# A hybrid layer with a mixture of experts on one core: shorter start, fewer small matrix products, zero rows sent in two parts, and another order of the last layer norm

## The chip, the core and the metric

The kernel runs on one core of one Trainium2 chip. The time is the device time of one execution in microseconds (us). The engines are named as the profile does: PE is TensorE, DVE is VectorE, ACT is ScalarE, POOL is GpSimd, SP is SyncE, which here only issues transfers. A transfer is issued on the queue of an engine and carried by the core's 16 DMA engines.

## The reference

One layer over T = 384 token rows of D = 1024, held as three tiles of 128: one tile is the context pass (stream 0), two are the sample (stream 1), to which a position embedding is added first. In short:

```python
sh1, sc1, g1, sh2, sc2, g2 = split(silu(c) @ w_ada + b_ada, 6)      # per stream
xs = x_sample + pos
z = (x * (1 + sc1) + sh1) @ w_in + b_in      # 11 groups of 512, and 16 gate columns
y_r = gelu(r_g) * (rglru forward + backward over conv(r_x))
y_h = head_rms(hgrn2 forward + backward(g_q, g_ff, g_fb, g_i)) * silu(g_o)
y_m = sigmoid(m_o) * head_ln(mlstm forward + backward(m_q, m_k, m_v, m_g))
x = layer_norm(ALPHA * x + g1 * (concat(y_r, y_h, y_m) @ w_out), ln1_g, ln1_b)
h = x * (1 + sc2) + sh2
f = sum over the 2 chosen of 16 experts: w * (silu(h @ w_gate) * (h @ w_up)) @ w_down
out = layer_norm(ALPHA * x + g2 * f, ln2_g, ln2_b)
```

The mLSTM needs, for each of 4 heads and 2 directions, the row of running maxima m_t over time, spread over all partitions. The expert stage takes each token row to two slots of a table `slot_rows` of 16 x 384 rows in DRAM; slots that no token takes must hold zeros. The final states of the three mixers are outputs too.

## The kernel before

**Large products.** All are made in three fp32r products: a weight piece of 512 columns, 2 MiB in DRAM, is split into w_hi (ACT, line 803 in the mixer, 1027 in the experts) and w_lo = w - w_hi (DVE, lines 1676 and 2130), 128x1024 at a time, and PE adds h_hi w_lo, h_lo w_hi and h_hi w_hi through the helper `mm` (line 1128). In the mixer the 24 pieces of `PIECES` pass through a ring of three slots, `ring`; SP sends a piece as soon as its slot is free (line 510). Pieces 0 and 1 are the ada groups 0 and 2 of w_ada (shift and scale of the first modulation), 2 is rx, 3 gq, 4 gff, and so on; 20 is mo, 21 to 23 are w_out.

**The order.** `schedule()` writes out a list of jobs; every engine walks through it and does its part of each job. So a job's place in the list sets what stands ahead of it on all of PE, ACT and DVE. The jobs that matter here:
- `ada_row g`: silu(c) times ada group g, 8 matmuls of 32x512 on PE (four column groups side by side, each over two of eight k), and one ACT copy to `ada_rows`; its four partial rows lie on different partitions.
- `ada_col g`: turns the row into columns and adds the partials: 4 matmuls of 128x2 with `stream_sel` (line 1128, out ps, in small,extra). There are 12 of these pairs.
- `xT i half`: PE transposes x (line 1244) for tile i; for the sample it waits for the position embedding, which DVE adds (line 1638, 128x2048).
- `h`, `tile k`, `first k`: DVE's columns of the modulation, ACT's modulated k-th eighth of hT (line 849), and the first part of rx.
- `gates`: the 16 gate columns, for y (i or f) and direction d 4 columns each: 32 matmuls of 4x384 at depth 128.
- `rows1`, `rows2`: DVE's work on the gate rows (36x384), with scans; it ends in the row of maxima, MR.
- `ml_rows n`: one matmul that spreads head h, direction d of MR over 128 partitions, plain fp32 with a depth of 4, eight of them.

**Zero rows.** SP sends 12 slices of 2 MiB from `zero_tile` to `slot_rows` (line 543) between pieces, as `ZERO_AFTER` says. ACT's job `take 6` overwrites the unit in which `zero_tile` lies, and waits for all twelve. POOL waits for all twelve before it scatters the token rows (six indirect DMAs, line 729).

**Small loads.** At the start POOL's queue carries x, pos and the gate weights ahead of the small weights of the RG-LRU. After the mixer POOL sends in one burst x again, pos, the rows of the second modulation, ln_g, ln_b, constants (`iota` last), and then, when the state C is out, the two g2 rows (512 KB each, line 705).

**The experts.** 16 experts run in pairs, 6 MiB of weights each; at the last one PE, ACT and DVE read `over` (how many rows the fullest expert has) and jump over two more passes that are not needed here.

**The tail.** ACT scales the rows that POOL has picked from the first of the two experts (line 1119); DVE adds the second and g2 (lines 2205 to 2207); for each tile PE mixes the last expert's rows with the picked ones into PSUM (from 740.60 us); DVE multiplies by g2 (line 2211), adds to x (2212), takes the statistics (1953, 1954), ACT takes a root (1122), DVE applies it (1956 to 1958), and SP sends the tile out.

## Time and profile before

| | us |
|---|---|
| median of 3 runs | 777.58 (777.57 to 777.61) |
| the profiled execution | 776.95 |
| its span, first to last instruction | 775.2 |
| PE busy | 703.2 (91%), mean granted clock 0.962 |
| DVE busy | 577.0 (74%) |
| ACT busy | 432.2 (56%) |
| POOL busy | 58.5 (8%) |
| moved by DMA | 220.06 MB, 284 GB/s |

The stages by time: start to 33, mixer to 345, out projection, first norm and routing to 441, experts to 736, tail to 775.2. Busy shares are averages over stages with different limits; the clock is given in parts of full speed.

### The profile page before, as it was taken

Reading aid. Unit: us, or ns where it says so; the run is one execution under the profiler, and the core shown is the slowest. Engines: PE = TensorE matmul, PEld = TensorE weight load, DVE = VectorE, ACT = ScalarE, POOL = GpSimd, SP = SyncE. Lnnn points to the kernel's source line nnn. Section 1 sums busy time; section 2 is a strip of 40 time slices with the busy share of each in tenths; the row PEclk is TensorE's granted clock in tenths of the full one; section 3 lists DMA queues with packets and bytes.
Section 4 is the critical chain, followed back from the end, with each engine's and each line's share of the span. In section 5 each row is a group of like instructions: output and inputs, shape, how many; then the busy total and the mean of one; then the engine's idle time right before and its main releaser. Section 6 shows DMA issues by size and latency. Waiting matters only on the chain.

```text
span 775.2 us, 12312 instructions
## 1 busy us (share of the span) xinstructions
PE 703.2 (91%) x4722; PEld 553.5 (71%) x4722; DVE 577.0 (74%) x834; ACT 432.2 (56%) x597; POOL 58.5 (8%) x90
## 2 busy tenths in 40 slices
PE   3699999799999989999996999999999999999870
PEld 1477998698778969884453877888888888788630
DVE  2549697667995344573596988998999998999675
ACT  1546867245124344761122368888888888888510
POOL 4050000000010000024000300000000000000400
PEclk9799999899999989999998899999999999999986
DMA  9995599989665650319704999999999999999521
GB/s 331 359 299 199 210 333 384 374 321 401 256 231 177 229 218 5 109 30 163 305 1 148 404 402 394 398 398 399 400 400 400 399 399 399 399 399 381 168 80 54
DMA packets 91507, 220.06 MB, mean 284 GB/s; under 512 B 3335, under 2 KB 3631, under 8 KB 91455
## 3 DMA queue, kind: packets, MB, share of 16 engines
q1 hardware_dynamic: 84512, 197.66, 68.2%
q0 software_dynamic: 6528, 21.56, 9.1%
q8 instruction: 33, 0.54, 0.3%
q10 hardware_dynamic: 415, 0.14, 0.1%
q14 instruction: 19, 0.16, 0.1%
HBM read 179.99 MB, written 39.36 MB: 283 GB/s over the span
## 4 chain that ended last, share of the span: by engine, by line
PE 68%; DVE 11%; DMA 9%; ACT 4%; issue 4%; POOL 2%; SPq 0%; DVEq 0%; ACTq 0%; POOLq 0%
PE ps L1128 65%; DMA ring<-in_w_ada 3%; DMA iota<-in_consts 3%; DMA arena<-in_w_up 2%; PE ps L1515 1%; DMA slot_rows<-arena,small 1%; PE ps L1534 1%; POOL slot_rows L729 1%; DMA ring<-in_w_gate 1%; ACT w_hi L1027 1%; DVE w_lo L1676 1%; ACT w_hi L803 1%; DVE small L1953 1%; DVE picked_rows L2211 1%; DVE arena L1957 1%
## 5 line engine op out<-in xcount | busy, mean ns | idle before, releaser
L2130 DVE TENSOR_TENSOR w_lo<-arena,w_hi 128x1024 fp32r<-128x1024 f32 x96 | 114.7, 1221 | 12.3 <-ACT w_hi L1027 11.5
L2130 DVE TENSOR_TENSOR w_lo<-ring,w_hi 128x1024 fp32r<-128x1024 f32 x96 | 114.8, 1221 | 9.3 <-ACT w_hi L1027 8.4
L1027 ACT ACTIVATE w_hi<-ring 128x1024 fp32r<-128x1024 f32 x96 | 100.5, 1063 | 21.7 <-PE ps L1128 18.9
L1027 ACT ACTIVATE w_hi<-arena 128x1024 fp32r<-128x1024 f32 x96 | 100.8, 1065 | 17.9 <-PE ps L1128 13.7
L1128 PE MATMUL ps<-h_hi,w_lo 128*128 128x384 f32 x288 | 103.6, 360 | 6.2 <-DVE w_lo L1676 4.7
L1128 PE MATMUL ps<-w_hi,slot_tokens_lo 128*128 128x512 f32 x256 | 102.6, 401 | 0.8 <-DVE w_lo L2130 0.8
L1128 PE MATMUL ps<-w_hi,slot_tokens_hi 128*128 128x512 f32 x256 | 100.2, 391 | 0.0
L1128 PE MATMUL ps<-w_lo,slot_tokens_hi 128*128 128x512 f32 x256 | 99.8, 390 | 0.0
L1128 PE MATMUL ps<-h_lo,w_hi 128*128 128x384 f32 x288 | 98.8, 343 | 0.0
L1128 PE MATMUL ps<-h_hi,w_hi 128*128 128x384 f32 x288 | 98.6, 342 | 0.0
L1676 DVE TENSOR_TENSOR w_lo<-ring,w_hi 128x1024 fp32r<-128x1024 f32 x44 | 53.7, 1225 | 30.1 <-ACT w_hi L803 29.0
L1128 PE MATMUL ps<-arena 128*32 128x32 f32 (+5 forms) x1576 | 61.7, 229 | 8.4 <-issue 7.4
L1128 PEld LDWEIGHTS ps<-h_hi,w_lo 128*128 128x128 f32 x288 | 55.9, 194 | 12.6 <-issue 9.3
L1128 PE MATMUL ps<-ring,arena 128*128 128x512 f32 x144 | 64.5, 607 | 0.0
L803 ACT ACTIVATE w_hi<-ring 128x1024 fp32r<-128x1024 f32 x44 | 46.1, 1051 | 33.0 <-PE ps L1128 32.1
L1128 PEld LDWEIGHTS ps<-arena 128*32 128x32 f32 (+3 forms) x1576 | 46.6, 123 | 22.5 <-issue 16.6
L875 ACT ACTIVATE arena<-ps,small 128x384 f32<-128x384 f32 x32 | 18.5, 579 | 71.9 <-PE ps L1128 71.8
L1128 PEld LDWEIGHTS ps<-h_lo,w_hi 128*128 128x128 f32 x288 | 56.2, 195 | 0.6
L1128 PEld LDWEIGHTS ps<-h_hi,w_hi 128*128 128x128 f32 x288 | 55.8, 194 | 0.0
L1128 PEld LDWEIGHTS ps<-w_hi,slot_tokens_lo 128*128 128x128 f32 x256 | 48.1, 188 | 10.8 <-issue 1.5
L1128 PEld LDWEIGHTS ps<-w_hi,slot_tokens_hi 128*128 128x128 f32 x256 | 48.0, 188 | 10.3
L1128 PEld LDWEIGHTS ps<-w_lo,slot_tokens_hi 128*128 128x128 f32 x256 | 48.2, 188 | 9.0
(352 smaller groups left out, 1115.9 us busy)
## 6 DMA issues: line engine op xcount, KB each, us to landing
slot_rows<-arena SPq DMA_DIRECT2D x12, 2048.0 KB, 17.0
ring<-in_w_in SPq DMA_DIRECT2D x11, 2048.0 KB, 11.5
ring<-in_w_ada SPq DMA_DIRECT2D x10, 2048.0 KB, 10.1
ring<-in_w_gate SPq DMA_DIRECT2D x8, 2048.0 KB, 18.3
ring<-in_w_up SPq DMA_DIRECT2D x8, 2048.0 KB, 19.2
ring<-in_w_down SPq DMA_DIRECT2D x8, 2048.0 KB
arena<-in_w_gate SPq DMA_DIRECT2D x8, 2048.0 KB, 18.4
arena<-in_w_down SPq DMA_DIRECT2D x8, 2048.0 KB, 15.1
```

The costliest lines, as they stand in the source:

```text
L729: pool.indirect_dma_start(slot_rows, bass.IndirectOffsetOnAxis(row_i[:, NT * c + i:NT * c + i + 1], 0), H2[:, i, :], None).then_inc(S["dis ...
L803: act.activation(part_unit(w_hi, u % 4, col), raw_unit(p % NSLOT, u % 4, col), ACT.Copy).then_inc(S["hi_ready"], 1)
L875: act.activation(chunk(dst_of[g], c), bank[:, 0:T], ACT.Gelu_apprx_tanh if g == "rg" else ACT.Identity, bias=bias).then_inc(S["z_taken"], 1)
L1027: act.activation(w_hi[:, at_ % 4, :], raw[:, q * QUARTER:(q + 1) * QUARTER], ACT.Copy).then_inc(S["hi_ready"], 1)
L1128: return pe.matmul(out, lhsT, rhs, start=start, stop=stop, skip_group_check=open_)
L1515: last = pe.transpose(ps[:, half, k * P:(k + 1) * P], XG[b][:, (4 * half + k) * P:(4 * half + k + 1) * P], ident)
L1534: last = pe.transpose(ps[:, 2, k * P:(k + 1) * P], AC[:, k * P:(k + 1) * P], ident)
L1676: tt(lo, raw, hi.bitcast(F32), ALU.subtract).then_inc(S["lo_dve"], 1)
L1953: step(dve.bn_stats(mv_stats[:, 6 * half:6 * half + 6], x[:, half * 512:(half + 1) * 512]))
L1957: step(stt(x, x, mv_stats[:, 12:13], ln_b[:, v, :], ALU.subtract, ALU.mult))
L2130: tt(w_lo[:, at_ % 4, :], raw[:, q * QUARTER:(q + 1) * QUARTER], w_hi[:, at_ % 4, :].bitcast(F32), ALU.subtract).then_inc(S["lo_dve"], 1)
L2211: step(tt(y[:, cols], ps[:, bank, :], g2_b[:, s, cols], ALU.mult))
```

## The change

1. **Start.** x, pos go on SP's queue behind piece 1; the gate weights go behind the small RG-LRU weights on POOL's. In `schedule()`, `ada_row 2`, both `ada_col` and `h 0` come ahead of the transposes; DVE adds pos in two halves behind `h 0`.
2. **Small products.** `ada_row` is 16 matmuls of 32x256, so that its partials lie on two column groups and two row groups; `ada_col` is 2 matmuls of 128x4. `gates 0` is 8 matmuls of 16x384 into four column groups, copied by ACT to `gate_sums`; `gates 1`, behind gq[0], adds and places them with 4 matmuls of 4x384. `ml_rows` is one fp32r matmul over `max_parts` (the maxima as a high and a low part, made by DVE at the end of rows2).
3. **Zero rows.** Five slices stay early and have a semaphore of their own, for which `take 6` waits; seven go out late, from `zero_late`, which POOL clears when the HGRN2 final state is done: one behind piece 20, two behind each w_out piece.
4. **g2.** The two g2 loads and the wait for C stand behind the six scatters.
5. **Tail.** `over` is read before the last down product; where no further pass is needed, ACT scales the picked rows ahead of the last expert's two output copies; the statistics are a sum that comes with the addition (DVE) and a square with a sum (ACT); the three tiles are interleaved. The job itself, mixing on PE, is as before.

The diff, cut:

```diff
-ZERO_AFTER = {4: 1, 6: 1, 8: 1, 9: 1, 10: 1, 11: 1, 12: 2, 13: 2, 14: 1, 15: 1}
+ZERO_AFTER = {4: 1, 6: 1, 8: 1, 15: 2}
+ZERO_LATE = {20: 1, 21: 2, 22: 2, 23: 2}
...
-    steps = [("cond",), ("ada_row", 0), ("rows",)] + [("xT", 0, half) for half in range(2)] + [("ada_row", 2)]
-    steps += [("xT", i, 0) for i in range(1, NT)] + [("ada_col", 0), ("ada_col", 2), ("h", 0)]
+    steps = [("cond",), ("ada_row", 0), ("rows",), ("ada_row", 2), ("ada_col", 0), ("ada_col", 2), ("h", 0)]
+    steps += [("xT", 0, half) for half in range(2)] + [("xT", i, 0) for i in range(1, NT)]
...
-    steps += [rx[0], rx[1], ("conv", 0), rx[2], rx[3], ("conv", 1), ("gates",), ("conv", 2)]
-    steps += [gq[0], ("lru_mm", 0), ("conv", 3), gq[1], ("lru_mm", 1), ("rows1",), gq[2], ("lru_act", 0), ("lru_den", 0)]
+    steps += [rx[0], rx[1], ("conv", 0), rx[2], rx[3], ("conv", 1), ("gates", 0), ("conv", 2)]
+    steps += [gq[0], ("gates", 1), ("lru_mm", 0), ("conv", 3), gq[1], ("lru_mm", 1), ("rows1",), gq[2], ("lru_act", 0), ("lru_den", 0)]
...
                     piece(n, ada_v[:, :, name * G:(name + 1) * G], KD)
+                    if n == 1:
+                        sp.dma_start(x_in[:, 0, :], a["x_prompt"][0]).then_inc(S["x_in"], 16)
+                        sp.dma_start(x_in[:, 1:3, :], a["x_sample"][0].rearrange("(i p) d -> p i d", p=P)).then_inc(S["x_in"], 16)
+                        sp.dma_start(pos_in, a["pos"].rearrange("(i p) d -> p i d", p=P)).then_inc(S["pos_in"], 16)
...
+            sp.wait_ge(S["zero_tile"], 2)
+            for _ in range(ZERO_LATE[20]):
+                zero_rows(zero_late, "in_zeroed")
             for n in range(3):
                 slot_free(WOUT[n])
                 piece(WOUT[n], a["w_out"][0, n * G:(n + 1) * G, :].rearrange("(k p) n -> p k n", p=P), C)
+                for _ in range(ZERO_LATE[WOUT[n]]):
+                    zero_rows(zero_late, "in_zeroed")
...
             pool.wait_ge(S["hg_final"], 1)
+            pool.memset(zero_late, 0.0).then_inc(S["zero_tile"], 1)
...
-            pool.wait_ge(S["out_C"], 16)
-            modulation([g2_b[:, s, :] for s in range(2)], 3, "g2_in")
-
-            pool.wait_ge(S["in_zeroed"], 16 * 12)
+            pool.wait_ge(S["zeroed_first"], 16 * ZERO_FIRST)
+            pool.wait_ge(S["in_zeroed"], 16 * (12 - ZERO_FIRST))
             pool.wait_ge(S["route_ready"], 1)
             for i in range(NT):
                 for c in range(2):
                     pool.indirect_dma_start(slot_rows, bass.IndirectOffsetOnAxis(row_i[:, NT * c + i:NT * c + i + 1], 0),
                                             H2[:, i, :], None).then_inc(S["dispatched"], 16)
+
+            pool.wait_ge(S["out_C"], 16)
+            modulation([g2_b[:, s, :] for s in range(2)], 3, "g2_in")
...
-                    for r in range(2):
+                    for kk in range(4):
                         for j in range(4):
-                            k = 4 * r + j
-                            last = mm(bank[32 * j:32 * j + 32, :], silu_w[:, 2 * k:2 * k + 32], w[k], r == 0, r == 1)
+                            k, cols = 4 * (j % 2) + kk, slice(256 * (j // 2), 256 * (j // 2) + 256)
+                            last = mm(bank[32 * j:32 * j + 32, 0:256], silu_w[:, 2 * k:2 * k + 32], w[k][:, cols], kk == 0, kk == 3)
...
-                    for c in range(4):
-                        last = mm(bank[:, 2 * c:2 * c + 2], ada_rows[:, b, c * P:(c + 1) * P], stream_sel)
+                    for x in range(2):
+                        last = mm(bank[:, 4 * x:4 * x + 4], ada_rows[:, b, x * P:(x + 1) * P], group_sel)
...
+                    if job[1] == 0:
+                        pe.wait_ge(S["gate_w_in"], 16)
+                        for r in range(2):
+                            for j in range(4):
+                                k = 4 * r + j
+                                last = mm(bank[32 * j:32 * j + 16, 0:T], gate_w[:, k, :], hT[:, k, :], r == 0, r == 1)
+                    else:
...
-                                last = mm(bank[at_:at_ + H, 0:T], gate_w[:, k, c0:c0 + H], hT[:, k, :], k == 0, k == KD - 1)
+                                last = mm(bank[at_:at_ + H, 0:T], ident_blocks[:, c0:c0 + H], gate_sums)
...
-                    r = slice(32 * d, 32 * d + H)
-                    mm(ps[:, 3, 0:T], ident[r, 32 * d + h:32 * d + h + 1].broadcast_to([H, P]), MR[r, :]).then_inc(S["bc_ready"], 1)
+                    mm(ps[:, 3, 0:T], row_sel[0:64 + HR, 4 * d + h:4 * d + h + 1].broadcast_to([64 + HR, P]),
+                       max_parts[0:64 + HR, :]).then_inc(S["bc_ready"], 1)
...
+                    step(dve.tensor_copy(max_hi, MR))
+                    step(tt(max_parts[64:64 + HR, :], MR, max_hi.bitcast(F32), ALU.subtract))
+                    step(dve.tensor_copy(max_parts[0:HR, :], max_hi.bitcast(F32)), "m_rows")
...
+            with act.Else():
+                first_picked()
+                out_rows_sb(NE - 1, NPAIR - 1, 1, True)
+            act.activation(rstd, eps, ACT.Sqrt)
             for i in range(NT):
                 act.wait_ge(S["ln_var"], NT + i + 1)
-                act.activation(rstd, mv_stats[:, 13:14], ACT.Sqrt, bias=eps).then_inc(S["ln_std"], 1)
+                act.activation(PICK[:, 1, i, :], X1[:, i, :], ACT.Square, bias=row_mean[:, i:i + 1], accum_out=row_sq[:, i:i + 1]).then_inc(S["ln_std"], 1)
+                act.wait_ge(S["ln_std"], NT + 2 * i + 1)
+                act.activation(row_rstd[:, i:i + 1], row_sq[:, i:i + 1], ACT.Sqrt, bias=eps, scale=1.0 / D).then_inc(S["ln_std"], 1)
...
+                step(stt(X1[:, i, :], X1[:, i, :], 1.0, y, ALU.mult, ALU.add, accum_out=row_mean[:, i:i + 1]))
+                step(ts(row_mean[:, i:i + 1], row_mean[:, i:i + 1], -1.0 / D, None, ALU.mult), "ln_var")
...
+                step(stt(x, x, row_mean[:, i:i + 1], ln_b[:, 2, :], ALU.add, ALU.mult))
+                step(dve.reciprocal(row_rstd[:, i:i + 1], row_rstd[:, i:i + 1]))
+                step(stt(x, x, row_rstd[:, i:i + 1], ln_b[:, 3, :], ALU.mult, ALU.add), "out_tile")
...
+            mixed_rows(0)
+            mixed_rows(1)
+            result(0)
+            mixed_rows(2)
+            result(1)
+            result(2)
```

How it moves instructions, at three places.

PE at the start of the program, before. `ring,silu_w` is an ada_row, `small,extra` are ada_col, line 1244 are transposes of x, `h_hi,w_lo` begins the large products:

```order
L1128 MATMUL ps<-ring,silu_w 32x512 x8
L1235 MATMUL ps<-small,arena 128x128
L1236 MATMUL ps<-small,arena 128x56
L1244 MATMUL ps<-small,arena 128x128 x8
L1128 MATMUL ps<-ring,silu_w 32x512 x8
L1244 MATMUL ps<-small,arena 128x128 x8
L1128 MATMUL ps<-small,extra 128x2 x8
L1128 MATMUL ps<-h_hi,w_lo 128x384
```

The same place now (line 1169 is `mm`, 1287 the transposes):

```order
L1169 MATMUL ps<-ring,silu_w 32x256 x16
L1276 MATMUL ps<-small,arena 128x128
L1277 MATMUL ps<-small,arena 128x56
L1169 MATMUL ps<-ring,silu_w 32x256 x16
L1169 MATMUL ps<-small,extra 128x4 x4
L1287 MATMUL ps<-small,arena 128x128 x16
L1169 MATMUL ps<-h_hi,w_lo 128x384
```

Both ada_row and ada_col now stand ahead of all transposes, which stand directly before the first large product.

SP late in the mixer, before. `slot_rows<-arena` is a slice of zero rows, the others are weight pieces:

```order
L510 DMA ring<-in_w_in 128x8x512
L543 DMA slot_rows<-arena 1024x1x512
L510 DMA ring<-in_w_ada 128x8x512 x3
L510 DMA ring<-in_w_in 128x8x512 x2
L510 DMA ring<-in_w_out 128x4x1024 x3
L554 DMA ring<-in_w_gate 128x8x512
```

And now:

```order
L521 DMA ring<-in_w_ada 128x8x512 x3
L521 DMA ring<-in_w_in 128x8x512 x2
L542 DMA slot_rows<-arena 1024x1x512
L521 DMA ring<-in_w_out 128x4x1024
L542 DMA slot_rows<-arena 1024x1x512 x2
L521 DMA ring<-in_w_out 128x4x1024
L542 DMA slot_rows<-arena 1024x1x512 x2
L521 DMA ring<-in_w_out 128x4x1024
L542 DMA slot_rows<-arena 1024x1x512 x2
L578 DMA ring<-in_w_gate 128x8x512
```

Seven slices now stand between and behind the three w_out pieces, the last two ahead of the first expert's weights.

POOL before the experts, before. `mod_rows` are the g2 rows, `slot_rows` the six scatters:

```order
L718 DMA b_router<-in_b_router 128x16
L719 DMA tri<-in_consts 128x128
L720 DMA desc_95<-in_consts 128x16
L721 DMA iota<-in_consts 128x128
L705 DMA arena<-mod_rows 128x1024 x2
L729 DMA slot_rows<-arena,small 6144x1024 x6
```

And now:

```order
L740 DMA b_router<-in_b_router 128x16
L741 DMA tri<-in_consts 128x128
L742 DMA desc_98<-in_consts 128x16
L743 DMA iota<-in_consts 128x128
L749 DMA slot_rows<-arena,small 6144x1024 x6
L727 DMA arena<-mod_rows 128x1024 x2
```

The two g2 loads have changed places with the six scatters.

## Rows read from the trace of the kernel before

**Rows 1.** Windows: us, busy (instructions) of each engine, PE clock, DMA share, GB/s

```profile
0.00:35.00 35.00, 14.87 (x73) 8.42 (x73) 11.30 (x23) 11.44 (x22) 7.83 (x16) 0.88 0.98 356
50.00:112.00 62.00, 60.73 (x378) 52.26 (x377) 51.72 (x109) 44.88 (x67) 0.56 (x1) 1.00 0.71 248
112.00:206.00 94.00, 86.50 (x1456) 75.40 (x1456) 70.80 (x100) 41.01 (x59) 0.00 (x0) 0.96 1.01 374
...
281.00:345.00 64.00, 61.39 (x366) 55.49 (x365) 38.97 (x94) 36.21 (x79) 5.86 (x17) 0.95 0.23 83
...
417.00:465.00 48.00, 38.76 (x221) 33.54 (x221) 41.51 (x84) 24.85 (x29) 7.54 (x6) 0.89 1.01 384
```

**Rows 2.** Chain that ended last, its start: start, us, what

```profile
1.33 20.70 DMA ring<-in_w_ada
...
31.48 1.24 DVE w_lo L1676
32.81 1.30 PE ps L1128 x3
```

**Rows 3.** Timeline, the start, DVE and PE: start, us, engine line, form

```profile
18.08 2.29 DVE L1638 TENSOR_TENSOR arena<-arena 128x2048 f32<-128x2048 f32 x1 [10.45 <-DMA arena<-in_pos]
...
24.85 1.90 PE L1244 MATMUL ps<-small,arena 128*128 128x128 f32 x8
```

**Rows 4.** PE: timeline (gates), groups (busy, mean ns), chain (111.83)

```profile
59.80 5.34 PE L1128 MATMUL ps<-arena 128*4 128x384 f32 x64
...
L1128 PE MATMUL ps<-small,extra 128*128 128x2 f32 x96 | 11.5, 243 | 0.8 <-issue 0.8
...
L1128 PE MATMUL ps<-arena,small 4*128 4x384 f32 x16 | 7.3, 532 | 1.7 <-ACT arena L977 1.7
...
111.83 8.22 PE ps L1128 x50
```

**Rows 5.** Stretch 60 to 112, DVE's timeline, and ACT's w_hi from the chain

```profile
61.24 1.23 DVE L1676 TENSOR_TENSOR w_lo<-ring,w_hi 128x1024 fp32r<-128x1024 f32 x1
...
89.36 0.56 DVE L1755 TENSOR_SCALAR arena<-arena 128x768 f32<-128x768 f32 x1 [5.38 <-ACT arena L904]
...
98.00 0.54 DVE L1840 TENSOR_TENSOR arena<-arena 36x384 f32<-36x384 f32 x1
...
83.52 1.05 ACT w_hi L803
```

**Rows 6.** PE's timeline in runs of small matmuls, and the window behind them

```profile
144.29 0.74 PE L1128 MATMUL ps<-arena 128*32 128x32 f32 x62 [1.99 <-issue]
...
150.06 0.86 PE L1128 MATMUL ps<-arena 128*32 128x32 f32 x46 [2.80 <-issue]
...
150.00:160.00 10.00, 9.94 (x177) 9.82 (x178) 4.03 (x5) 1.59 (x3) 0.00 (x0) 0.69 1.03 371
```

**Rows 7.** The window of late w_out pieces, and the zero slices' issues (to landing)

```profile
320.00:345.00 25.00, 25.00 (x159) 22.85 (x158) 16.86 (x47) 17.27 (x35) 2.59 (x7) 1.00 0.25 85
...
slot_rows<-arena SPq DMA_DIRECT2D x12, 2048.0 KB, 17.0
```

**Rows 8.** Chain that ended last, before the experts

```profile
440.46 10.98 DMA slot_rows<-arena,small
```

**Rows 9.** The tail: ACT's and PE's timeline, and DVE's part of the chain

```profile
740.08 1.15 ACT L1119 ACTIVATE picked_rows<-picked_rows,small 128x1024 f32<-128x1024 f32 x1 [2.51 <-issue]
...
754.89 1.02 PE L1128 MATMUL ps<-expert_out,arena 128*128 128x512 f32 x2
...
759.16 1.30 DVE arena L1958
...
763.19 0.71 DVE small L1953
...
765.48 1.30 DVE arena L1957
...
766.80 1.28 DVE arena L1958
```

More of the change, by code:

```diff
@@ L370, in build @@
         zero_tile = unit(11, 1024, 512)
+        zero_late = unit(6, 1024, 512)
         YR, YH, YM = unit(13), unit(14), unit(10)
@@ L381, in build @@
         FE, BR = [unit(2, T * n, T)[0:HR, :] for n in range(2)]
-        MR = unit(3, 1024, T)[0:HR, :]
+        gate_sums = unit(0, 2 * T, T)
+        MR_all = unit(3, 1024, T)
+        MR = MR_all[0:HR, :]
         CR, NBM = GI, FE
@@ L526, in _, with zero_rows @@
             zeroed = [0]
+            def zero_rows(tile, name):
+                rows = NE * ROOM // 12
+                dst = slot_rows[zeroed[0] * rows:(zeroed[0] + 1) * rows, :].rearrange("(p a) (b n) -> p (a b) n", p=P, n=512)
+                sp.dma_start(dst, tile.unsqueeze(1).broadcast_to([P, rows // P * 2, 512])).then_inc(S[name], 16)
+                zeroed[0] += 1
             for n, (what, name) in enumerate(PIECES):
@@ L853, in _ @@
                     act.wait_ge(S["rows_zeroed"], 1)
-                    for y in range(2):
+                    if job[1] == 0:
+                        act.activation(gate_sums, bank[:, 0:T], ACT.Identity).then_inc(S["z_taken"], 1)
+                    for y in range(2 * job[1]):
                         for d in range(2):
@@ L1242, in _ @@
                         pe.wait_ge(S["pos_added"], 1)
+                    if i == 1 and half == 1:
+                        pe.wait_ge(S["pos_added"], 2)
                     for k in range(4):
@@ L1707, in _ @@
                     modulated(job[1])
+                    if job[1] == 0:
+                        dve.wait_ge(S["x_in"], 32)
+                        dve.wait_ge(S["pos_in"], 16)
+                        for half in range(2):
+                            cols = slice(512 * half, 512 * half + 512)
+                            step(tt(x_in[:, 1:3, cols], x_in[:, 1:3, cols], pos_in[:, :, cols], ALU.add), "pos_added")
                 elif kind == "tile":
@@ L1827, in _ @@
                 elif kind == "rows1":
-                    taken_by_act(("gates",))
+                    taken_by_act(("gates", 1))
                     dve.wait_ge(S["gate_rows"], 3)
@@ L1947, in _ @@
             step(stt(chunk(YM, H - 1), ps[:, 2, 0:T], colsA[:, A_MLG + H - 1:A_MLG + H], chunk(MO, H - 1), ALU.mult, ALU.mult), "ym_done")
-            def norm(i, v, n, last="dve"):
-                x = X1[:, i, :]
-                for half in range(2):
-                    step(dve.bn_stats(mv_stats[:, 6 * half:6 * half + 6], x[:, half * 512:(half + 1) * 512]))
-                step(dve.bn_aggr(mv_stats[:, 12:14], mv_stats[:, 0:12]), "ln_var")
-                dve.wait_ge(S["ln_std"], n + 1)
-                step(dve.reciprocal(rstd, rstd))
-                step(stt(x, x, mv_stats[:, 12:13], ln_b[:, v, :], ALU.subtract, ALU.mult))
-                step(stt(x, x, rstd, ln_b[:, v + 1, :], ALU.mult, ALU.add), last)
             def with_cols(dst, src, cols):
@@ L2176, in expert_pass @@
                 expert(base, 0, 0 if base else 5)
+                over = dve.value_load(over_i[0:1, 0:1], min_val=0, max_val=T) if base == 0 else None
                 expert(base + 1, 1)
@@ L2190, in expert_pass @@
                     lo(n, 8 + q, down, q)
[L2192 to L2193 removed]
+                return over
+            over = expert_pass(0)
             with dve.If(over > P):
@@ L2199, in _, with mixed_rows @@
             dve.wait_ge(S["g2_in"], 16 * 2)
-            for i in range(NT):
-                s = min(i, 1)
-                y = PICK[:, 0, i, :]
-                if i == 0:
-                    dve.wait_ge(S["picked_scaled"], 1)
-                    step(stt(y, PICK[:, 1, i, :], pick_e[:, 1, i:i + 1], y, ALU.mult, ALU.add))
-                    step(tt(y, y, g2_b[:, s, :], ALU.mult))
-                    step(tt(X1[:, i, :], X1[:, i, :], y, ALU.add))
+            dve.wait_ge(S["picked_scaled"], 1)
+            first = PICK[:, 0, 0, :]
+            step(stt(first, PICK[:, 1, 0, :], pick_e[:, 1, 0:1], first, ALU.mult, ALU.add))
+            step(tt(first, first, g2_b[:, 0, :], ALU.mult))
+            step(tt(X1[:, 0, :], X1[:, 0, :], first, ALU.add))
+            def mixed_rows(i):
+                y = PICK[:, 0, i, :]
                 for half, bank in enumerate(MIX_BANKS[i]):
```

93 lines of the change are left out of this document (54 added, 39 removed).

## The prediction

> **What bounds the kernel now.** I read five views of the profiled execution, in this order: the page's busy shares, then a table by stage, then the chain of work that ended last, then timelines of the places that the diff touches, then the table of DMA issues. The page shows TensorE (PE) busy nearly throughout. The stages show where it is not: in 50 to 112 us it is busy 60.73 of 62, in 112 to 206 it loses 7.5 of 94, in 281 to 345 some 2.6 of 64, in 417 to 465 some 9 of 48; in the first 35 us it is busy for 14.87 only [rows 1], and the last 40 us are mostly another engine's [rows 9]. So from 33 to 735 us a microsecond taken from PE's own instructions is worth nearly a microsecond, unless ACT, DVE or the DMA engines are close behind. They are close in two stages: after 417 us the DMA engines are at 1.01, and in 50 to 112 us DVE is busy 51.72 of 62.
>
> At the start the chain is a DMA that lands at 22.03, then PE, then ACT and DVE, until the first large product at 32.81, right behind the w_lo that starts at 31.48 and takes 1.24 [rows 2]. At the end it is DVE: three output tiles one behind the other [rows 9].
>
> All terms below are against the profiled execution (span 775.2, its time 776.95); the median of the three runs is 777.58, so 0.6 us is added back at the end.
>
> **The start.** Before, x and pos are loaded on POOL's queue beside the two ada pieces, so the second ada piece lands at 22.03. After, SP sends ada 0, ada 2, x, pos and only then rx. Ahead of rx's end are 2 + 2 + 1.5 + 1 + 2 = 8.5 MiB, 8.9 MB; at the 356 GB/s of the first 35 us [rows 1] that is 25.0 us, with the start of 1.33 it lands near 26.3. Behind it come one w_hi rounding (1.05 us, [rows 5]) and one w_lo (1.24, [rows 2]): 28.6. The other way in: 6.5 MiB (x and pos too) are there at 20.5; the pos addition, 2.29 us in one piece before [rows 3], ends near 22.9; 24 transposes in groups of 8 that take 1.90 at this clock [rows 3] run on PE from x's landing, the last group after the addition, ready near 26; then ACT's and DVE's share of the first tile give 28 or a little more. ada_row 2 and the two ada_col are off that path, being done by about 19. So the first product is near 28.5 instead of 32.81: **+4.3**. If the queue runs slower because all loads share one it is 2; if the small loads left out of the sum cost nothing and the clock is already up it is 5.5.
>
> **gates.** Before, 64 records take 5.34 us from 59.80 on [rows 4]. After, they are 8 matmuls of 16x384 over the full depth (16 records) and, after the first gq unit, 4 more: 24 records of the same 384 columns, again in four column groups side by side. At 5.34/64 they are 2.0 us: saved 3.3. But DVE is not idle in this stretch; and its w_lo comes close. The w_lo that PE uses next, at 65.1, is ready at 61.24 + 1.23 [rows 5]; with 3.3 less PE would want it at 61.8. I take **+2.6**, with 0.7 and 3.3 as ends. ACT gets one eviction more; it is busy 44.88 of 62 there [rows 1].
>
> **rows1 and rows2.** DVE gets one 128x384 operation in rows1 and three of 36x384 in rows2. rows1 is followed by an idle time of 5.38 on DVE [rows 5]: nothing. rows2 starts at 98.00, in the chain that runs through DVE to PE's 111.83 [rows 4, 5]. A 36x384 operation takes 0.55 there, a copy with one input I put at three quarters of it: 0.55 + 2 x 0.4 = 1.3, less some slack: **-1.2**, between 0 and -1.65.
>
> **ada_col.** Twelve of them are 96 records and 11.5 us [rows 4], 0.96 each. A record takes 243 ns though it has 2 columns, so the columns are not what it costs. After, each is 4 records of 128x4: near half, 0.43 with the overlap at the ends taken off. Of the 12, two lie in the start's slack, ten on PE between 42 and 281: **+4.3**. Ends: 2 (if PE is held by others half of the time) and 4.8. ada_row keeps its columns (16 of 256 for 8 of 512) but has twice the records. Where it stands alone this is free; inside the stretch of missing time below it brings instructions: **-0.8**, between 0 and -2.
>
> **ml_rows.** Eight of these stand between 285 and 340. The 16 records, with a depth of 4 in plain fp32, take 7.3 us [rows 4], 0.91 each time and some 0.83 without the overlap. After, each is one fp32r matmul of 128x384; 50 of those take 8.22 [rows 4], 0.17 each. 8 x 0.66: **+5.3**. PE idles 2.6 of 64 there [rows 1], so I keep 3 as the lower end.
>
> **Fewer zero slices early.** In 112 to 206 PE shows gaps with no releaser, the largest 1.99 and 2.80 [rows 6], all in runs of small 32x32 matmuls, while the DMA engines are at 1.01 [rows 1]. Behind the second gap the clock is 0.69 in 150 to 160 [rows 6], which is the lower level for over half of it. The reading: PE's own instruction blocks (an instruction queue is among the page's DMA queues) come late behind 2 MiB writes. The seven slices that leave it and its neighbours are 14.7 MB beside the 374 GB/s x 94 us = 35 MB moved there. With over half of the load still there, the blocks have more room in part of the stretch only: **+1.7**. Ends: 0 and 10 (all 7.5 of the idle time and 2.5 of clock). The Trainium skill, Runtime: NRT & Kernel Launch, Instruction fetch mechanics, says that instruction blocks are fetched ahead, in order, and that the fetch is hidden by the issue floor. By that rule the relief is 0 and the time 762.0; the two gaps speak against it.
>
> **The late slices.** 14.7 MB between 265 and 345. The DMA share is 0.25 in 320 to 345 [rows 7] with a w_out piece in it, and nobody waits for those. The last pair goes with the third w_out piece: 6.3 MB, 16.4 us at 384 GB/s [rows 1], and so done inside that stretch if the piece is sent near its start. POOL waits for them only at the dispatch, a little before 440.46 [rows 8]. **0**.
>
> **The g2 loads.** Before they are the last of the burst that POOL sends after the mixer. After, they come behind the six scatters, the last of which is sent at 440.46, in a stretch at 384 GB/s where the chain waits 10.98 for a scatter's landing [rows 8] and then for w_up. 1.05 MB there is 2.7 us of all engines: **-2.6**. In exchange the burst is 1 MiB shorter, but behind it PE has the out projection to work on, so that gives nothing. Ends: 0 (if w_up wins) and -6 (the clock, 0.89 over 417 to 465 [rows 1], falls once more in the longer wait).
>
> **The tail.** ACT scales the first picked rows at 740.08, 1.15 long, after two output copies and 2.51 of issue [rows 9]. After, it does so before the copies, when its last rounding is done, by about 734; so DVE's three operations on them, some 3.8 us, end before the first mixed bank. PE still takes a branch behind its last product; mixing starts near 740.2. Its last group starts at 754.89 [rows 9]; it ends near 755.3 then, 754.9 after. A tile takes DVE 7.64 (759.16 to 766.80), of which 2.29 (763.19 to 765.48) are the statistics and the wait for ACT's root [rows 9]. After, the mean comes with the sum, and ACT's square (1.15, as its 1024 wide operation above) and root run under other work of DVE: 7.64 - 2.29 + 0.15 = 5.5 a tile. PE becomes the bound: from 754.9 come the rest of tile 2 (0.7 + 1.3 + 0.2), result 1 and result 2 (1.30 + 1.28 + 0.2 each [rows 9]) and 0.5 of hand-overs: 763.2 to 764.6. The last operation ended at 768.08: **+3.7**; ends 2 and 5.
>
> **Sum.** 4.3 + 2.6 - 1.2 + 4.3 - 0.8 + 5.3 + 1.7 - 2.6 + 3.7 = 17.3. 776.95 - 17.3 = 759.65 profiled; as a median 777.58 - 17.3 = **760.3**.
>
> **Rivals.**
> First, the relief is whole: every gap in 112 to 206 goes, and with them the low clock at 150 to 160. That is 5.8 more of idle time and up to 2.5 of clock: about 753.5 (752 to 756). For it: the gaps have no other releaser. Against: weight pieces still fill the engines for half of the time there. Chance 0.25.
> Second, PE's savings are taken up by its neighbours. DVE holds PE at the gates (0.7 for 2.6), half of ada_col goes into waits (2.1 for 4.3) and the g2 loads cost a low clock as well (-5 for -2.6): 6.5 less, about 766.8 (764 to 770). For it: DVE's 51.72 of 62 and the clock of 0.89 behind 417 [rows 1]. Chance 0.20.
> Third, slower: each late slice lands at the median of the early ones, 17.0 us [rows 7], one after another. Seven are 119 us, from 265 to 384: they then share the burst of 345 to 385, on whose last transfer DVE waits, and the first expert pieces come after them; 35 us later, less the savings: about 795. It decides if slices are still in flight when the burst (which is behind 345) begins. Against it: 17.0 is the time to landing in a full queue, of several at once. Chance 0.03.
> Fourth, the edits do what they say but the savings come to no more than 1.6 us, for instance because expert weights, at full DMA rate from 417 on, set the end whatever comes before. About 777. Against: those transfers start when the w_out pieces free the ring, so they come earlier too. Chance 0.02.
>
> **Numbers.** The likeliest case has 0.50, with 757 to 764. The range 753 to 768 takes in most of the first and second rival. A measurement of this kernel can tell 0.2% (1.6 us) from no change: faster 0.95, same 0.02, slower 0.03.
>
> **What would show it.** First large product at 28.5; PE's gates in two groups of 2.0 us together; ada_col 0.4; ml_rows 0.17 to 0.2; gaps in 112 to 206 near 5.8 us in all instead of 7.5; the stretch from the scatters to the first expert longer by 2.6; 5.5 us from one output tile to the next. A gap left at the first product, a DMA share at 1.0 when the burst begins, or an expert period other than 18 us would make it wrong.

## The result: 750.13 us, 3.5% faster, and past the low end of the range

The changed kernel takes 750.13 us (median of four, 748.04 to 752.23) against 777.6 before; the ratio is 0.965, with an interval of 0.963 to 0.967. The forecast was 760.3, range 753 to 768: the sign was right, the gain was 27.5 us where I had 17.3. The profiled execution was the slowest of the four: it took 752.23 us, with a span of 750.5. Against the profiled execution of before (776.95, span 775.2) it gained 24.7 us, so the tables below account for 24.7 and not for all of the 27.5.

The same table by stage of after (us, busy and instructions of PE, PEld, DVE, ACT, POOL, then the PE clock, the DMA share, GB/s), beside [rows 1]:

```profile
0.00:35.00 35.00, 16.28 (x108) 11.40 (x109) 15.10 (x32) 12.77 (x24) 4.93 (x12) 0.81 0.97 359
...
50.00:112.00 62.00, 59.17 (x361) 53.20 (x360) 54.09 (x113) 42.95 (x63) 2.25 (x3) 1.00 0.81 279
112.00:206.00 94.00, 90.96 (x1736) 78.97 (x1735) 79.79 (x111) 42.34 (x60) 0.00 (x0) 1.00 0.61 214
...
281.00:345.00 64.00, 62.64 (x336) 50.50 (x336) 39.78 (x108) 33.99 (x64) 15.09 (x31) 1.00 0.79 234
...
417.00:465.00 48.00, 44.55 (x218) 36.33 (x217) 39.06 (x47) 31.36 (x39) 3.83 (x5) 0.96 1.04 398
```

The third row is the news: in 112 to 206 the DMA engines are at 0.61 instead of 1.01, PE's clock is full, and PE works off 1736 records in the time in which it did 1456. Some of these records are the doubled ones of ada_row. The stages shift, so fixed windows don't say what each gained. For that I follow one and the same instruction through both traces. Before, from PE's timeline and the chain, are the first token product, the first ml_rows, the first product of the routing, the first transposes for an expert, and the last expert product (the first large product and the one at 111.83 stand in [rows 2, 4]):

```profile
190.78 0.47 PE L1128 MATMUL ps<-w_hi,h_lo 128*128 128x512 f32 x1
...
272.72 0.58 PE L1128 MATMUL ps<-arena,small 4*128 4x384 f32 x1
...
426.38 1.90 PE ps L1128 x8
...
467.12 1.09 PE L1515 MATMUL ps<-small,extra 128*128 128x128 f32 x8 [0.93 <-DMA extra<-slot_rows]
...
736.05 0.40 PE L1128 MATMUL ps<-w_hi,expert_act_hi 128*128 128x512 f32 x1
```

The same of after, with the first large product ahead and DVE's last operation behind:

```profile
29.34 0.66 PE L1169 MATMUL ps<-h_hi,w_lo 128*128 128x384 f32 x1 [4.50 <-DVE w_lo L1729]
...
108.03 0.41 PE L1169 MATMUL ps<-h_hi,w_lo 128*128 128x384 f32 x1 [0.67 <-DVE w_lo L1729]
...
177.01 0.47 PE L1169 MATMUL ps<-w_hi,h_lo 128*128 128x512 f32 x1
...
256.88 0.42 PE L1169 MATMUL ps<-max_parts,row_sel 100*128 100x384 f32 x1
...
404.96 1.90 PE ps L1169 x8
...
448.68 1.97 PE L1566 MATMUL ps<-small,extra 128*128 128x128 f32 x8 [2.60 <-DMA extra<-slot_rows]
...
718.28 0.39 PE L1169 MATMUL ps<-w_hi,expert_act_hi 128*128 128x512 f32 x1
...
742.01 1.28 DVE arena L2274
```

Between these instructions the two traces take (us; the last column has the parts of my sum that fall into the stretch):

| stretch | before | after | gained | my terms for it |
|---|---|---|---|---|
| to the first large product | 32.81 | 29.34 | 3.5 | start 4.3 |
| to the piece at 111.83 | 79.0 | 78.7 | 0.3 | gates 2.6, rows2 -1.2, ada_col some 0.9 |
| to the first token product | 79.0 | 69.0 | 10.0 | gaps 1.7, ada_row -0.8, ada_col some 2 |
| to the first ml_rows | 81.9 | 79.9 | 2.1 | ada_col some 1.5 |
| to the routing | 153.7 | 148.1 | 5.6 | ml_rows 5.3 |
| to the first expert transposes | 40.7 | 43.7 | -3.0 | g2 -2.6 |
| to the end of the last expert product | 269.3 | 270.0 | -0.7 | 0 |
| to the end of the span | 38.8 | 31.8 | 6.9 | tail 3.7 |

The gains add up to 24.7 where my terms have 17.3. Two stretches hold the error: the third has 7 us more than its terms, the last 3 more; the second has 2 less.

### The profile page after: what moved, and what is told of

It is laid out like the page before. It is cut to its first block, busy times and chain, and to the rows that moved or that the text cites. A ratio compares the mean times of both kernels' runs of the same rounds, so it can differ in the third digit from the quotient of the medians.

```text
span 750.5 us, 12527 instructions
## 1 busy us (share of the span) xinstructions
PE 684.4 (91%) x4818; PEld 550.6 (73%) x4818; DVE 575.3 (77%) x838; ACT 433.5 (58%) x605; POOL 57.8 (8%) x88
## 4 chain that ended last, share of the span: by engine, by line
PE 66%; DVE 15%; DMA 9%; ACT 4%; issue 3%; SPq 1%; POOL 1%; DVEq 0%; ACTq 0%; POOLq 0%
PE ps L1169 63%; DMA ring<-in_w_in 3%; DMA extra<-slot_rows 2%; DMA arena<-in_pos 2%; PE ps L1566 2%; DVE w_lo L1729 2%; DMA slot_rows<-arena,small 2%; DVE arena L1884 1%; DVE arena L1883 1%; DVE arena L1829 1%; PE ps L1585 1%; POOL slot_rows L749 1%; DMA ring<-in_w_gate 1%; ACT w_hi L826 1%; SPq L550 1%
## 5 line engine op out<-in xcount | busy, mean ns | idle before, releaser
L1169 PE MATMUL ps<-h_hi,w_lo 128*128 128x384 f32 x288 | 102.0, 354 | 9.4 <-DVE w_lo L1729 6.0
L1169 PE MATMUL ps<-arena 128*32 128x32 f32 (+5 forms) x1528 | 56.5, 220 | 3.1 <-issue 1.5
L902 ACT ACTIVATE arena<-ps,small 128x384 f32<-128x384 f32 x32 | 18.5, 579 | 68.8 <-PE ps L1169 68.8
L1169 PE MATMUL ps<-w_hi,expert_act_lo 128*128 128x512 f32 x128 | 51.8, 405 | 2.7 <-DVE expert_act_lo L2199 1.4
## 6 DMA issues: line engine op xcount, KB each, us to landing
ring<-in_w_up SPq DMA_DIRECT2D x8, 2048.0 KB, 18.5
```

The source lines that it names most:

```text
L902: act.activation(chunk(dst_of[g], c), bank[:, 0:T], ACT.Gelu_apprx_tanh if g == "rg" else ACT.Identity, bias=bias).then_inc(S["z_taken"], 1)
L1169: return pe.matmul(out, lhsT, rhs, start=start, stop=stop, skip_group_check=open_)
```

## The experiments

The kernel before was run beside each; its medians were 776.5 to 778.8 us, with single runs from 773.6 to 781.2. The edits below are the parts of the diff that stands ahead of the prediction; a diff is shown only where there is something else.

### The late slices alone

```diff
-ZERO_AFTER = {4: 1, 6: 1, 8: 1, 9: 1, 10: 1, 11: 1, 12: 2, 13: 2, 14: 1, 15: 1}
+ZERO_AFTER = {4: 1, 6: 1, 8: 1, 15: 2}
+ZERO_LATE = {20: 1, 21: 2, 22: 2, 23: 2}
...
+            pool.wait_ge(S["zeroed_first"], 16 * ZERO_FIRST)
+            pool.wait_ge(S["in_zeroed"], 16 * (12 - ZERO_FIRST))
             pool.wait_ge(S["out_C"], 16)
             modulation([g2_b[:, s, :] for s in range(2)], 3, "g2_in")
-            pool.wait_ge(S["in_zeroed"], 16 * 12)
```

> The kernel before with the zero rows alone changed: five slices early, seven late. Since the second zero block lies where the g2 rows go, POOL waits for the late slices before it loads them (still ahead of the scatters). With the small products alone, 764.74, a gap of 3.50 and a clock of 0.66 in 145 to 150 stayed. Theory 1: the DMA load makes the gaps, and the late slices alone remove gaps (4.8 of 7.5 us) and low clock (3.1): 6 to 8 us faster, about 770. Theory 2: slices matter only together with the products: at most 2 us, about 776.

769.21 us against 776.48, ratio 0.991 (0.988 to 0.993). The stretch to the first token product is 70.5 us (112.85 to 183.39) instead of 79.0. The run of block products in which the two large gaps stood before, first its other rows in the kernel before (those behind the gaps are [rows 6]):

```profile
140.98 1.31 PE L1128 MATMUL ps<-arena 128*32 128x32 f32 x130
...
144.87 1.92 PE L1128 MATMUL ps<-ring,silu_w 128*32 128x512 f32 x16
146.58 0.67 PE L1128 MATMUL ps<-arena 128*32 128x32 f32 x50
```

and then with the late slices alone:

```profile
141.98 1.31 PE L1142 MATMUL ps<-arena 128*32 128x32 f32 x131
143.64 0.73 PE L1142 MATMUL ps<-arena 128*32 128x32 f32 x61 [0.35 <-issue]
...
147.21 0.60 PE L1142 MATMUL ps<-arena 128*32 128x32 f32 x46 [0.61 <-issue]
```

The gaps sit at the same places of the program but are 0.35 and 0.61 instead of 1.99 and 2.80. From one to the next there are 62 + 16 + 50 = 128 matmuls before, each with its weight load: 256 instructions, done in about 3 us. The low clock is gone as well: 1.00 in 150 to 155, where it was 0.50. One large gap is left, against the expectation: 1.77 us ahead of 195.63, when the two slices behind piece 15 are under way and the DMA share is 1.02 (190 to 195). Theory 1 holds: this edit alone is worth 8.4 us in its stretch, 7.3 in the whole.

### The small products alone

> The kernel before with the small products alone changed (gates, ada_row, ada_col, ml_rows). Theory 1 (the slices made the gaps): the gaps at 142 to 150 and the low clock stay, and the gain is that of the products alone: 4.3 + 5 + 1.5, less what ada_row adds: 9 to 10 us, about 768. Theory 2 (the products made them go): gaps gone, 16 us or more, about 761.

764.74 us against 777.08, ratio 0.984 (0.981 to 0.987): 12.3 us. A large gap is still there, one of 3.50 instead of two of 1.99 and 2.80, and the DMA engines before it are full:

```profile
145.72 1.33 PE L1135 MATMUL ps<-arena 128*32 128x32 f32 x95 [3.50 <-issue]
...
125.00:140.00 15.00, 15.00 (x236) 13.69 (x238) 10.27 (x17) 8.19 (x13) 0.00 (x0) 1.00 1.05 403
```

So the products did not take the load's gap away. That it is 12.3 and not 9 to 10 lies between the theories. The stretch to the first token product shrinks by 4.5 (109.90 to 184.38). Of this, ada_col is about 2 by my terms and 1.3 is idle time in large gaps (3.50 for 1.99 and 2.80). The rest I can't put down to a cause from one profile.

### The changed kernel with all slices early

> The changed kernel with all twelve slices of zero rows early again, from one block, as before; everything else as changed. The late slices alone took 8.4 us off the stretch from the 14th piece's first product to the first token product (78.96 to 70.54), the products alone 4.5 (to 74.48), both and the rest 10.0 (to 68.98). So undoing the slices here should give that stretch back 5.5 (74.5), with gaps of over 2 us in the runs of 32x32 products: 755 to 756. Rival: with fewer records the blocks are asked for less often, and the slices cost less than 3 us: 752.

757.88 us, against 750.41 for the changed kernel repeated (below): 7.5 more, and 2 above what I had expected. The two were measured beside different repetitions of the kernel before (776.99 and 776.48); set against these it is 7.0 more. The stretch is 74.9 us (107.14 to 182.05), as expected, and the gap is back:

```profile
142.98 1.50 PE L1155 MATMUL ps<-arena 128*32 128x32 f32 x95 [3.49 <-issue]
```

The slices are worth about the same with the products changed or not: 7.0 to 7.5, and 7.3.

### Two slices at another moment

```diff
-ZERO_AFTER = {4: 1, 6: 1, 8: 1, 15: 2}
+ZERO_AFTER = {4: 1, 6: 1, 8: 1, 11: 2}
```

> The changed kernel with g2 ahead of the scatters, and the two slices that stood behind piece 15 (sent at 178.6) behind piece 11 instead (sent near 128.4): the same five early and seven late. The run of 130 small products ends at 139.5 in both. Theory 1 (blocks late while the DMA engines are full): 6 MiB are then under way from 128 to about 144, so the gap at 139.5 grows from 0.6 to 2 us or more, low clock behind it, and the piece that went out at 139.6 lands later; the gap near 197 shrinks or stays: 2 to 4 us slower than the same kernel without the move. Rival (the sum of bytes in the mixer matters, not their moment): no difference, and a gap near 0.6 at 139.5.

751.31 us against 747.93 for its base on the same chip: 3.4 more, for two slices that go out 50 us earlier and are otherwise the same. PE's timeline and the window of this kernel:

```profile
140.44 0.19 PE L1169 MATMUL ps<-arena 128*32 128x32 f32 x1
143.53 1.15 PE L1169 MATMUL ps<-arena 128*32 128x32 f32 x95 [2.88 <-issue]
...
140.00:145.00 5.00, 2.12 (x110) 1.78 (x102) 2.44 (x4) 0.39 (x1) 0.00 (x0) 0.92 1.05 402
```

and of its base:

> The changed kernel with g2 ahead of the scatters, once more, beside the one above, as its base: 748 us, gap 0.6 at 139.5.

```profile
139.45 0.19 PE L1169 MATMUL ps<-arena 128*32 128x32 f32 x1
139.96 1.02 PE L1169 MATMUL ps<-arena 128*32 128x32 f32 x95 [0.30 <-issue]
...
135.00:140.00 5.00, 4.70 (x237) 3.83 (x237) 3.97 (x4) 1.81 (x3) 0.00 (x0) 1.00 0.05 17
```

At the same instruction the wait is 2.88 us with the DMA share at 1.05, and 0.30 when it has just been 0.05. What counts is the load at the moment of the gap, not the bytes of the stretch.

The traces also show what PE waits for. Instructions come to an engine by DMA, in blocks, and the profile counts a queue for them; on the page of before it is

```profile
q8 instruction: 33, 0.54, 0.3%
```

that is 33 packets of 16 KiB. The trace has the time of each packet. Beside the gaps shown above they are (us; "goes on" is the start of PE's next product):

| kernel | gap | packet begins | lands | PE goes on | behind the landing |
|---|---|---|---|---|---|
| before | 1.99 | 141.78 | 142.88 | 144.29 | 1.41 |
| before | 2.80 | 147.85 | 148.78 | 150.06 | 1.28 |
| late slices alone | 0.35 | 141.22 | 142.31 | 143.64 | 1.33 |
| late slices alone | 0.61 | 144.74 | 145.94 | 147.21 | 1.27 |
| late slices alone | 1.77 | 193.28 | 194.22 | 195.63 | 1.41 |
| small products alone | 3.50 | 143.25 | 144.25 | 145.72 | 1.47 |
| all slices early | 3.49 | 140.48 | 141.48 | 142.98 | 1.50 |
| two slices moved | 2.88 | 141.31 | 142.25 | 143.53 | 1.28 |
| its base | 0.30 | 137.77 | 138.70 | 139.96 | 1.26 |

Every one of these gaps ends 1.26 to 1.50 us behind the landing of an instruction block, long or short. The packet itself takes about as long at the long gaps (0.93 to 1.10 us) as at the short ones (0.93 to 1.21): what differs is when it begins. In the kernel before PE goes on at 144.29 and the next packet begins 3.56 us later, at a DMA share of 1.02; with the late slices alone it goes on at 143.64 and the next packet begins 1.10 us later, at 0.07.

### The start alone

> The kernel before with the start alone changed (x and pos on SP's queue, order of the jobs, gate weights later). The first large product stands at 29.34 in after against 32.81. If nothing later takes that back: 3.5 us faster, about 774.1. Rival: DVE, without idle time in 50 to 84, takes part of it back behind the later pos addition: 1 to 2 us, about 776.

775.6 us against 777.08, ratio 0.997 (0.995 to 0.999), ten runs in two groups, 772.1 to 772.6 and 775.2 to 777.2. The trace has the first large product at 29.48, as expected. The ends of the interval allow 0.5 to 4 us, so the times don't tell the two theories apart. The trace, which is of an execution of the faster group (772.57), speaks for the first: of the 3.3 us at the first product 2.9 are still there at the product that stood at 111.83 (now 108.93).

### The tail, whole and in halves

> The kernel before with the tail alone changed. After shows 24.6 us from PE's last expert product to the last output operation, before 31.6. If that is the tail's own: 7 us faster, about 770.6, with PE's mixing at the upper level of the clock and DVE the bound. Rival: the clock at which PE mixes depends on the run and not on this edit: mixing at half clock and 4 us, about 773.5, as I forecast.

768.85 us against 777.08, ratio 0.989 (0.985 to 0.992): 8.2 us; 6.8 of them lie behind the last expert product.

> The kernel before with the last layer norm alone restructured and interleaved; ACT's scaling, the reading of over and PE's branch stay as before. The whole tail alone gave 768.85. Theory 1: the norm removes DVE's part (7.64 to 5.5 a tile) but PE still mixes after 4.15 us at half clock and is then the bound: last bank about 755.9, end 4 us earlier, about 773.5, as in my forecast for the tail. Theory 2: the norm is all of it, PE's clock is of no weight: 7 us, about 770.5.

773.02 us against 776.48, ratio 0.995 (0.993 to 0.997): 3.5 us. This is the tail as I had forecast it.

> The kernel before with the other half of the tail: over is read before the last down product, ACT scales the picked rows first; the last norm as before. The whole tail took 6.8 us off (38.75 to 31.9 from PE's last expert product to the end of the span), the norm alone 3.75 (35.0). If the halves add: 3 us here, PE's mixing 2.4 us behind its last product and DVE the bound. Rival: the norm's gain needs the earlier PE, and this half alone gives 4 us or more, since DVE's first three operations leave its chain too (3.8 us): tail near 34.5.

771.78 us against 776.99, ratio 0.993 (0.990 to 0.996): 5.2 us, so the rival. PE's first mixing product, in the norm alone, the branch alone, both, and after:

```profile
742.75 1.19 PE L1134 MATMUL ps<-expert_out,arena 128*128 128x512 f32 x1 [4.26 <-issue]
...
736.40 1.10 PE L1139 MATMUL ps<-expert_out,arena 128*128 128x512 f32 x2 [1.77 <-ACT expert_out L1057]
...
738.34 2.80 PE L1145 MATMUL ps<-expert_out,arena 128*128 128x512 f32 x4 [2.37 <-issue]
...
720.82 3.34 PE L1169 MATMUL ps<-expert_out,arena 128*128 128x512 f32 x4 [2.15 <-issue]
```

With `over` read ahead of the last down product the wait before mixing falls from 4.15 to about 2. The branch itself still costs its time on PE's sequencer: 5.49 us from 734.94 on before, 4.35 from 716.30 on after. But it begins earlier, beside the last products; in both kernels mixing starts 0.17 us behind its end. The edit holds one thing more, which the list of changes leaves out: PE's first mixing product waits for the first of the last expert's two output copies and no longer for both. No run has it alone. In the traces of before, of the branch alone, of both and of after, the copies are done before the branch ends; in the repetition below it is the first copy that releases mixing, and waiting for both would have cost about half a microsecond more. And the clock: over ten us from the first mixing product it is 0.66 before (740 to 750) and 0.83 after (721 to 731).

### The g2 loads

> The changed kernel with the two g2 loads ahead of the scatters again, behind the wait for the zero rows. In after the distance from the mask product to the first expert transposes is 43.7 us, before 40.7. If the g2 loads cost that: 3.0 us faster than after, about 747. Rival: the 3 us come from the shifted prefetch of the expert weights (the out projection ends earlier, the same bytes are still to be moved): no gain, 750.

748.19 us, 2.2 less than the changed kernel in the same set (750.41).

> The kernel before with the two g2 loads alone moved behind the scatters. The changed kernel with them ahead again took 40.93 us from the mask product to the first expert transposes instead of 43.72. Expected: 40.74 becomes 43.5, some 3 us slower, about 779.5. Rival: in the kernel before they displaced others in the burst, so a part comes back before the mask product: 1.5 us slower or less.

780.99 us against 776.99, ratio 1.007 (1.005 to 1.009): 4.0 slower. The routing's first product to the first expert transposes is 43.5 (425.17 to 468.67), as expected. The last us come behind it. The transposes of this kernel, and the window in which they lie:

```profile
468.67 1.53 PE L1515 MATMUL ps<-small,extra 128*128 128x128 f32 x8 [3.62 <-DMA extra<-slot_rows]
...
465.00:475.00 10.00, 6.38 (x28) 5.49 (x28) 6.55 (x7) 7.17 (x10) 0.00 (x0) 0.83 1.04 396
```

and the window of after behind its wait of 2.60 at the same place:

```profile
450.00:455.00 5.00, 5.00 (x23) 4.27 (x22) 5.00 (x6) 4.76 (x9) 0.00 (x0) 0.84 1.04 406
```

Where the g2 loads come late, PE waits 2.6 to 3.8 us for the expert's rows (3.77 with all slices early; 0.93 before), and its clock falls behind that wait.

### The changed kernel again, and two more slices late

> The changed kernel once more, the same file. Its four times lay in two pairs, 748.0 to 748.5 and 751.8 to 752.2, and so did those of the start alone (772.1 to 772.6 and 776.0 to 777.2). If the pairs are the clock's falls at different places, the profile of a run of the shorter kind lacks one stretch of low clock, by 3 to 4 us, most likely 268 to 275 or 360 to 365.

750.41 us (750.08 to 753.07). The profiled execution, with a span of 748.3, has its low clock at 264 to 275 as the first one had, but none at 355 to 370. That window of after, and of the repetition:

```profile
355.00:370.00 15.00, 14.37 (x48) 7.49 (x47) 10.86 (x12) 2.55 (x4) 0.00 (x0) 0.89 0.19 73
...
355.00:370.00 15.00, 14.75 (x53) 7.78 (x52) 10.81 (x13) 2.66 (x4) 0.00 (x0) 1.00 0.15 58
```

So the same program loses some 1.7 us to the clock here in one execution and not in the other. It loses as much elsewhere: at 264 to 275 the clock is 0.70 in the repetition and 0.84 in the first, and from the first ml_rows to the routing both take the same time (148.0 and 148.1). The mean granted clock of the two is 0.964 and 0.965. So the low clock moves from place to place; it does not explain the pairs.

It moves over a border of my table too. In the repetition the clock is 0.71 in 710 to 715, among the last expert products, and mixing then starts 0.78 us behind the last of them, released by ACT's copy: the stretch up to that product takes 273.0 instead of 270.0, and the tail 28.7 instead of 31.8. Together they take the same (301.7 and 301.8; 308.1 before).

```diff
-ZERO_AFTER = {4: 1, 6: 1, 8: 1, 15: 2}
-ZERO_LATE = {20: 1, 21: 2, 22: 2, 23: 2}
+ZERO_AFTER = {4: 1, 6: 1, 8: 1}
+ZERO_LATE = {20: 3, 21: 2, 22: 2, 23: 2}
```

> The changed kernel with the g2 loads ahead of the scatters and two more slices moved: three stay early, nine go late (three behind piece 20, two behind each w_out piece). With the late slices alone a gap of 1.77 stood at 193.86, just when the two slices behind piece 15 went out (185.8 and 190). If DMA load makes the gaps it goes, and this is 1 to 1.5 us faster than with g2 alone (748.2): about 747. Rival: the burst at 335 to 385 now meets slices in flight, iota lands later and it is slower.

748.69 us (746.83 to 749.74), no faster than with g2 alone (748.19 and 747.93). With the late slices alone the gap of 1.77 stood under full DMA engines; this kernel has them empty there. The window of each, and the one wait of PE in the second:

```profile
190.00:200.00 10.00, 8.23 (x121) 6.46 (x120) 9.58 (x15) 1.06 (x1) 0.00 (x0) 0.83 1.04 373
...
190.00:200.00 10.00, 8.56 (x225) 6.80 (x227) 9.62 (x14) 2.12 (x2) 0.00 (x0) 1.00 0.01 2
...
198.99 1.03 PE L1169 MATMUL ps<-arena 128*32 128x32 f32 x96 [1.44 <-DVE arena L1885]
```

These are two different waits. The 1.77 us stood inside a run of block products, had no releaser and ended behind an instruction block (above). The 1.44 us stand ahead of such a run and are released by an operation of DVE (line 1885), and DVE is busy 9.6 of 10 us there. The base of this kernel has the same wait for DVE (1.27 at 196.87) and between 170 and 200 no other over 0.3: the gap that I wanted to take away was in the kernel before with late slices, not in this one, so there was nothing to gain. Nine late slices didn't disturb the burst. The fastest version measured is the changed kernel with the g2 loads ahead of the scatters: 747.9 to 748.2.

## Why the prediction was wrong

**Fewer zero slices early: the term that failed.** I had +1.7 with ends of 0 and 10 and took a value near the low end, because over half of the bytes stay in the stretch. It is 7.0 to 7.5. The reading was right (instruction blocks that come late behind full DMA engines), and the rival that has the relief whole (753.5, a chance of 0.25) was the one to take, for this term: it adds 6.8 to my sum. The time lies below that rival's range too, since the tail gave more as well. The step that failed was from bytes to relief ("with over half of the load still there, the blocks have more room in part of the stretch only"). A gap doesn't shrink with the mean load; the large ones are 1.8 to 3.5 us when the engines are full at their moment, and at the same places of the program 0.3 to 0.7 when they are not, and seven slices fewer leave pauses between the weight pieces, of which the block runs near 140 now meet one. The Trainium skill (Runtime: NRT & Kernel Launch, Instruction fetch mechanics) has blocks of 16 KiB, 256 instructions, fetched in order. The 128 matmuls and weight loads between two gaps agree with that size. What the Trainium skill says in the same section, that the fetch is hidden, doesn't hold here: 2.88 against 0.30 us at one instruction. That it is the fetch, and not another thing that full engines delay on PE's side, the packets show: each gap ends 1.26 to 1.50 us behind the landing of a block. What holds a packet back before it begins, a place in a queue or a late request, the trace doesn't tell.

**The tail: 6.9 for 3.7** in the table, and 8.2 for the tail alone by the medians. The norm was sized right (3.5 alone). The step that failed is "PE still takes a branch behind its last product; mixing starts near 740.2". The branch was there, but moving the read of `over` ahead of the last down product let it begin beside the products: mixing starts 2.15 us behind the last product instead of 4.15. With the shorter wait more of the mixing ran at the upper level of the clock. PE's last mixing product ended 16.1 us behind the last expert product, where the sum had 18.5 (754.9 less 736.45), so PE was no longer the bound that I had put in: from 729.73 on the chain is DVE's alone. I had also misread a row: the last group of before starts at 754.89 and takes 1.02, so it ends at 755.9 and not near 755.3.

**The start: 3.5 for 4.3.** Three rows of the chain and PE's timeline of after:

```profile
1.94 3.94 SPq L550
...
7.96 18.88 DMA ring<-in_w_in
...
22.91 1.94 PE L1287 MATMUL ps<-small,arena 128*128 128x128 f32 x8 [2.86 <-DVE arena L1766]
```

rx landed at 26.84, where I had 26.3, and the first w_lo ended at 29.3, where I had 28.6. rx was sent only at 7.96, because the issues of x and pos held SP's queue for 5.9 us. That does not explain the half microsecond by itself: the DMA engines were full all the while (a share of 1.05 in 4 to 6 us, 1.07 in 6 to 8), and in the kernel before the third issue of this queue, rx itself, took 7.86 us from 1.94 on. In both kernels it is the third issue that is long, whatever it issues.

**Gates and rows2: 0.3 for 1.4 and the ada_col in it.** The groups of PE's small products in after (busy, mean ns):

```profile
L1169 PE MATMUL ps<-small,extra 128*128 128x4 f32 x48 | 6.4, 239 | 0.6 <-issue 0.5
...
L1169 PE MATMUL ps<-max_parts,row_sel 100*128 100x384 f32 x8 | 3.4, 425 | 2.2 <-ACT arena L1004 2.2
L1169 PE MATMUL ps<-arena 128*16 128x384 f32 x16 | 1.5, 489 | 0.0
L1169 PE MATMUL ps<-arena,small 128*4 128x384 f32 x8 | 0.8, 486 | 0.0
```

The sizes are right: gates 2.3 where I had 2.0, ada_col 5.1 us less in all for the 5.2 expected, ml_rows 3.9 less in busy time. But up to 108 us PE was not the only bound: in this stretch its busy time falls by 3.2 us (77.7 to 74.5) and the length by 0.3, so what it saved went into waits. Rows of PE's and of DVE's timeline:

```profile
102.44 0.41 PE L1169 MATMUL ps<-h_hi,w_lo 128*128 128x384 f32 x1 [1.35 <-ACT small L866]
...
99.71 0.35 DVE L1919 CAST max_hi<-arena 36x384 fp32r<-36x384 f32 x1
100.10 0.55 DVE L1920 TENSOR_TENSOR max_parts<-arena,max_hi 36x384 fp32r<-36x384 f32 x1
100.69 0.35 DVE L1921 CAST max_parts<-max_hi 36x384 fp32r<-36x384 f32 x1
```

PE waits 1.35 us at 102.44, where it had no such wait, and rows2 is longer by what I had put. This is what the second rival said, for this stretch alone.

**ml_rows 5.6 for 5.3, g2 -3.0 for -2.6** were right within half a microsecond. For ml_rows that is in part luck: at full clock the time from one to the next falls by 0.85 to 0.88 us in four of seven cases (7.64 to 6.79, for one), where I had 0.66, and the last of them grows by 0.7 for a reason that I don't know. The g2 term lacks the low clock behind the wait, some 1 us, which its lower end had. **The late slices cost nothing**, as forecast: the stretch that has them is no longer than with all slices early (148.1 and 149.4).

## What to carry to other kernels

Where an engine runs through many short instructions, look for gaps without a releaser, and count the instructions from one to the next; if the DMA engines are full there, and the packets of the instruction queue land just ahead of each gap's end, moving bulk writes to a quiet stretch can give back most of the gap and the clock behind it, so price that by the gap and not by the share of bytes. Put the read of a value that a branch needs ahead of the last long work, so that the branch is done beside it. An issue can hold its queue for microseconds while the transfers ahead of it fill the engines (7.86 and 3.94 us here); look whether the engines were full before you call that a cost. Before you repair a gap, find it in the trace of the kernel that you are going to change.

## What the runs showed of the hardware that I had not expected

A stretch of 256 PE instructions that is worked off in about 3 us waits 1.8 to 3.5 us for its next block of 16 KiB while the DMA share is 1.0, and 0.3 to 0.7 when it has just been low (2.88 and 0.30 at the same instruction); PE goes on 1.26 to 1.50 us behind the block's landing in either case. The branch on `over` holds PE's sequencer for 4.35 us in after and 5.49 before; in the repetition it takes 4.19, ends 0.25 us behind the last product and ahead of ACT's copy, and so holds nothing up. Two runs of one program have their low clock at different places (0.89 and 1.00 in 355 to 370, 0.84 and 0.70 in 264 to 275) at the same mean (0.965 and 0.964); the single times of one kernel lie up to 8 us apart (773.6 to 781.2), which is more than the smaller terms of a sum like this one.
